# Prompt attention of a one-core hybrid trunk: probabilities scaled before their transposition, values as the stationary operand

## The chip, the cores and the metric

The program runs on one core of a Trainium2 chip. The metric is the time of one execution on the device, in microseconds. The engines of the core are named as the profile names them: PE (TensorE, matrix multiplications and transpositions), DVE (VectorE), ACT (ScalarE), POOL (GpSimd) and SP (the queue that loads the weights). Each runs its own list of instructions in order, and they meet only at semaphores.

## The reference

One layer of a decoder: 512 prompt tokens and 8 sample tokens go through a combined input projection, four mixers (gated linear attention, HGRN2, pooling, sparse attention), gates, an output projection and an MLP. The change lies in the sparse attention of the prompt, and in how its result is handed to the last branch projection:

```
q = rms_norm(heads(nq, H_D), q_ng).reshape(B, L, KVH_D, G_D, HD_D)     # 2 key heads x 4 queries x 64
pc    = masked_softmax(q kc^T, ...);  o_cmp = pc vc                    # 31 compressed blocks
ps    = masked_softmax(q ks^T, ...);  o_slc = ps vs                    # selected blocks
pw    = masked_softmax(q kw^T, ...);  o_win = pw vw                    # window
return gb[..., 0:1] * o_cmp + gb[..., 1:2] * o_slc + gb[..., 2:3] * o_win
...
x = x + einsum(sum_b sigmoid(h W_g + b_g)_b * (o_b W_b), w_out)        # o_nsa is branch b = 3
```

With 512 prompt tokens there are 8 selection blocks, fewer than the 16 to be chosen, and the window is as long as the prompt, so both branches are plain causal attention with their own keys and values.

## The kernel before

All matrices are float32. A projection of the layer is made of three float32r products (high and low parts of weight and input); ACT casts the high part of each 128 x 1024 weight chunk (`upper`, L1151) and POOL subtracts to get the low part (`lower`, L2072). DVE and ACT take the results out of PSUM.

**Compressed branch** (PE L865 to L882). The scores of four query tiles lie in `CM`, 128 x 1024. DVE subtracts the maximum, ACT takes the exponential, DVE sums (L1751), masks with `cmp01` (L1752, which signals `cp`), and afterwards forms 1/sum times the gate in `rsc` (L1754, L1757). PE waits for `cp`, transposes each tile and multiplies it with the block-diagonal compressed values `VBK`: the transposed probabilities are the stationary operand, 256 columns of values move (L878). DVE scales the result with `rsc` on its way from PSUM into `ON`, token-major (L1767).

**The prompt loop.** `PAIRS` (L472) lists 32 pairs: query tile i = 0..3 (the outer loop), branch b (selected, window), and n = 0..3, which stands for two heads, 7-n (key head 1, c = 0) and n (key head 0, c = 1). The loop runs 34 rounds; round p works on three pairs at once:

- PE: a step of the compressed attention of the samples (`compressed_step`); scores of pair p (L972, two heads on two row halves, 128(i+1) columns); then for c = 0, 1: transposition of the probabilities of pair p-1 (`probs_transposed`, L943, i+1 tiles into bank 4), one step of the branch and gate projections (`mix_step`, L809, into the only bank 7), and the product of probabilities and values of pair p-2 (`probs_values`, L956).
- DVE: causal mask (L1888) and maximum (L1890) of pair p; for c = 0, 1 the copy of the transposed probabilities of pair p-1 out of PSUM into `PT` (L1899) and the evacuation of the mix step if it is a branch step (L1676, L1680).
- ACT: the exponentials of pair p with their row sums into `rs` (L1350), then the mix steps of the round: tanh of a gate (L1299) and `upper` of the next chunk (L1151).
- POOL: `lower` after each `upper`, and the gathers of the compressed cache (L2143).

Of every four rounds, the first two hold gate steps (24 matmuls each) and the last two branch steps (12 each). An `upper` falls into three of every four rounds, always beside the round's first mix step: behind its tanh in the second round of the four, right behind the exponentials in the third and fourth. For p below 8 the mix steps also carry the folds of the gathered compressed cache (DVE L1686, L1687, PE L822).

**The product with the values** takes the transposed probabilities (128 keys x 128 tokens) as the stationary operand and 128 columns of values as the moving one, so bank 6 holds eight heads side by side, token-major. The probabilities aren't normalised: after every four pairs (p % 4 == 1, L1906) DVE takes the reciprocal of the row sums, multiplies by the gate (L1909, L1910), scales bank 6 into `TQ` (L1915) and adds it to `ON` (L1916), which signals `on`. The next four pairs may write bank 6 only behind it.

**After the loop** PE waits for the last `on`, transposes `ON` in 16 matmuls (L987), DVE copies them into the feature-major `ONT` (L1919), PE fills a bank with sample values (L994), waits for all four copies, and begins the cache attention of the samples (`keys_transposed`, L1008; `scores`, L1018; `values`, L1039). POOL may gather piece 7 and later of that cache only behind the last `on` (L2168).

## Time and profile before

| | |
|---|---|
| runs | 1409.42, 1410.96, 1417.57 us; median 1410.96 |
| profiled execution | 1409.77 us, of which the span in the profile is 1408.0 us |
| granted PE clock, mean | 0.963 of full speed |
| busy share of the span | PE 91%, DVE 40%, ACT 30%, POOL 36% |
| prompt loop | first scores at 545.78 us, last product with values begins at 817.37 us |
| cache attention of the samples | 825.48 to about 893 us |

The profile is of one execution. Busy time of PE counts overlapping matmuls in a pipeline, so the rate at which matmuls follow each other is read from a run of them: start of the first to end of the last, less the length of one, divided by their number less one. A float32 product is issued as two matmuls.

### The profile page before, as it was taken

To read this page: it belongs to the slowest core of one execution; us is meant where nothing else is said; L and a number is where in the kernel's file an instruction comes from. 1 tells how busy PE (TensorE), PEld (TensorE's weight loads), DVE (VectorE), ACT (ScalarE), POOL (GpSimd) and SP (SyncE) were. 2 spreads that over 40 slices of the span, in tenths; PEclk is the share of its full clock that TensorE was granted. 3 is DMA by queue.
4 is the path that set the end of the run, shared out by engine and by line. 5 is a ranking of instruction groups with operands and counts; after the bars stand their busy time and mean duration, and the time that the engine had idled before them with its cause. 6 is when DMAs were issued, how large, how long until landed. Compare 5 with 4: busy or idle time off the path is not lost.

```text
span 1408.0 us, 24162 instructions
## 1 busy us (share of the span) xinstructions
PE 1279.7 (91%) x10332; PEld 1196.6 (85%) x10332; DVE 568.7 (40%) x853; ACT 416.4 (30%) x647; POOL 502.5 (36%) x262
## 2 busy tenths in 40 slices
PE   4898989998987898888998977889999999999998
PEld 3798888897977887777887855889999999999998
DVE  3544644262425553656667655623122100122002
ACT  3343321013443112223332213333343311234110
POOL 1355533055123334322221235234334444444441
PEclk9899999999998899999999999999999999999999
DMA  4221010632024354431110349232222222222222
GB/s 170 106 91 46 31 60 31 134 96 100 31 92 135 124 177 147 138 105 46 46 61 31 120 160 328 88 130 90 75 89 91 86 94 89 90 90 89 90 90 75
DMA packets 47159, 139.51 MB, mean 99 GB/s; under 512 B 4454, under 2 KB 16074, under 8 KB 46682
## 3 DMA queue, kind: packets, MB, share of 16 engines
q1 hardware_dynamic: 36706, 100.50, 21.5%
q0 software_dynamic: 10368, 37.75, 7.9%
q8 instruction: 68, 1.11, 0.3%
q14 instruction: 17, 0.14, 0.0%
HBM read 129.98 MB, written 8.49 MB: 98 GB/s over the span
## 4 chain that ended last, share of the span: by engine, by line
PE 74%; DVE 12%; DMA 4%; ACT 3%; issue 3%; POOL 2%; DVEq 0%; ACTq 0%
PE PS L598 42%; PE PS L809 10%; PE PS L626 7%; DMA M<-cache_cmp_kv,idx 2%; PE PS L680 2%; PE PS L956 2%; POOL WL L2072 1%; DMA M<-cache_slc_kv,idx 1%; PE PS L943 1%; DVE M L1686 1%; PE PS L1008 1%; PE PS L972 1%; DVE xT L1560 1%; PE PS L584 1%; PE PS L772 1%
## 5 line engine op out<-in xcount | busy, mean ns | idle before, releaser
L2072 POOL TENSOR_TENSOR WL<-M,WH 128x1024 fp32r<-128x1024 f32 x159 | 392.7, 2473 | 759.9 <-ACT WH L1151 759.6
L1151 ACT CAST WH<-M 128x1024 fp32r<-128x1024 f32 x159 | 165.7, 1047 | 280.4 <-DMA M<-weights 280.4
L598 PE MATMUL PS<-hH,WH 128*128 128x260 f32 x1040 | 216.3, 290 | 14.5 <-DVE hL L1448 12.9
L598 PE MATMUL PS<-hL,WH 128*128 128x260 f32 x1040 | 212.6, 287 | 0.0
L598 PE MATMUL PS<-hH,WL 128*128 128x260 f32 x1040 | 212.4, 286 | 0.0
L598 PEld LDWEIGHTS PS<-hH,WH 128*128 128x128 f32 x1040 | 164.1, 193 | 18.8 <-POOL WL L2072 7.6
L598 PEld LDWEIGHTS PS<-hL,WH 128*128 128x128 f32 x1040 | 163.9, 193 | 0.0
L598 PEld LDWEIGHTS PS<-hH,WL 128*128 128x128 f32 x1040 | 163.6, 192 | 0.0
L809 PE MATMUL PS<-hH,WH 128*128 128x260 f32 x384 | 115.6, 301 | 4.4 <-ACT tmp L1299 2.4
L809 PE MATMUL PS<-hL,WH 128*128 128x260 f32 x384 | 111.3, 290 | 0.0
L809 PE MATMUL PS<-hH,WL 128*128 128x260 f32 x384 | 110.9, 289 | 0.0
L598 PE MATMUL PS<-uH,WH 128*128 128x260 f32 x512 | 103.2, 283 | 2.3 <-DVE M L2046 2.3
L598 PE MATMUL PS<-uH,WL 128*128 128x260 f32 x512 | 103.2, 283 | 0.0
L598 PE MATMUL PS<-uL,WH 128*128 128x260 f32 x512 | 103.0, 283 | 0.0
L626 PE MATMUL PS<-WH,hH 128*128 128x256 f32 (+1 forms) x280 | 85.0, 304 | 4.6 <-POOL WL L2072 3.7
L809 PEld LDWEIGHTS PS<-hH,WH 128*128 128x128 f32 x384 | 75.7, 197 | 7.6 <-ACT tmp L1299 4.8
L598 PEld LDWEIGHTS PS<-uH,WH 128*128 128x128 f32 x512 | 78.9, 188 | 2.7 <-issue 2.7
L626 PE MATMUL PS<-WL,hH 128*128 128x256 f32 (+1 forms) x280 | 80.6, 288 | 0.0
L2054 DVE TENSOR_TENSOR M<-M,PS 128x520 f32 x16 | 11.1, 697 | 171.7 <-PE PS L598 171.7
L626 PE MATMUL PS<-WH,hL 128*128 128x256 f32 (+1 forms) x280 | 80.3, 287 | 0.0
L598 PEld LDWEIGHTS PS<-uH,WL 128*128 128x128 f32 x512 | 78.9, 188 | 0.0
L598 PEld LDWEIGHTS PS<-uL,WH 128*128 128x128 f32 x512 | 78.7, 188 | 0.0
(371 smaller groups left out, 2340.8 us busy)
## 6 DMA issues: line engine op xcount, KB each, us to landing
M<-weights SPq DMA_DIRECT2D x159, 512.0 KB, 3.2
M<-cache_win_kv POOLq DMA_DIRECT2D x7, 512.0 KB, 4.3
spill<-xT SPq DMA_DIRECT2D x1, 2080.0 KB, 8.7
M<-spill SPq DMA_DIRECT2D x1, 2080.0 KB, 8.7
M<-x_prompt SPq DMA_DIRECT2D x4, 512.0 KB
y_prompt<-M SPq DMA_DIRECT2D x4, 512.0 KB
con<-tables SPq DMA_DIRECT2D x1, 1437.5 KB, 12.4
M<-state_gla SPq DMA_DIRECT2D x2, 512.0 KB, 6.6
```

Source lines behind the costliest of these rows:

```text
L584: last = mm(PS[:, bank + h, 0:HALF], ones, SQN[k % 2][:, HALF * h:HALF * h + HALF], start=(k == 0), stop=(k == KT - 1))
L598: last = mm(PS[:, bank + h, 0:HALF], w[:, slot_of(n), k, :], x[:, HALF * h:HALF * h + HALF], start=(start and k == k0 and w is WH and x is ...
L626: last = mm(PS[0:m, bank, 0:pieces * cols], x[:, k, t], w[:, n % 4:n % 4 + pieces, k, 0:cols], start=(k == 0 and x is hH and w is WH), sto ...
L680: last = mm(PS[:, bank, 64 * k:64 * k + 64], a, later, start=True, stop=True)
L772: last = mm(PS[:, 2 * (e % 2) + h, 0:HALF], ones if kind == "o" else BO, SQ[e % 2][:, HALF * h:HALF * h + HALF], start=True, stop=True)
L809: last = mm(PS[:, mix_bank(k), 0:HALF], w[:, slot_of(n), at, :], x[:, half], start=(c == 0 and w is WH and x is hi), stop=(c == (KT if gat ...
L943: last = tr(PS[:, 4, 128 * j:128 * j + 128], P[2 * (p % 2) + c][:, 128 * j:128 * j + 128], ident)
L956: last = mm(PS[:, 6, out], PT[2 * (p % 2) + c][:, j], zt[:, j, col:col + out.stop - out.start], start=(j == 0), stop=(j == i))
L972: last = mm(PS[:, 2 * (p % 2) + c, 0:128 * i + 128], QT[r, g, 128 * i:128 * i + 128], (KTS, KTW)[b][r, 0:128 * i + 128], start=True, stop= ...
L1008: last = tr(PS[:, s % 2, 128 * i:128 * i + 128], piece(j, s, i)[0], ident)
L1151: nc.scalar.copy(WH[:, at].rearrange("p k n -> p (k n)"), WR[:, at]).then_inc(sem("w_hi"), 1)
L2072: p.tensor_tensor(WL[:, at].rearrange("p k n -> p (k n)"), WR[:, at], WH[:, at].rearrange("p k n -> p (k n)"), ALU.subtract).then_inc(sem( ...
```

## The change

The row sums of a pair are turned into gate / sum at once, for its two heads, by DVE (`probs_factor`, two small instructions a round). ACT multiplies each head's probabilities by that factor in place (`ACT.Copy` with a per-partition scale, two a round, behind the round's first mix step), and signals `p_norm`, for which the transposition now waits. In the product the values become the stationary operand (128 keys x 64) and the transposed probabilities move; head 7-n writes partitions 64 to 127 of bank 6 and head n partitions 0 to 63, on two column groups of PE, and the matmuls of the two heads alternate. All eight pairs of a query tile, both branches, accumulate in bank 6, feature-major, and DVE adds the bank to `ONT` once per query tile. The compressed branch is treated likewise: `CM` is scaled with `rsc` ahead of `cp`, the product writes feature-major on two column groups in 8 products of 128 columns a tile, and DVE copies it into `ONT`. `ON`, `TQ`, the 16 transpositions and the four copies behind the loop go. The order of the features in `ONT` is another, so the rows of `w_branch[3]` are reordered on the host, and the samples' result goes into `ONT` in two copies, not four.

```diff
@@ PE, compressed branch
-                    for k in range(HKV):
-                        last = mm(PS[:, i - 1, 256 * k:256 * k + 256], PTC[:, i - 1, k], VBK[:, k],
-                                  start=True, stop=True)
+                    for g in range(G):
+                        for k in range(HKV):
+                            last = mm(PS[64 * k:64 * k + 64, i - 1, 128 * g:128 * g + 128], VBK[:, k, 64 * g:64 * g + 64],
+                                      PTC[:, i - 1, k], start=True, stop=True)
@@ PE, prompt loop
             def probs_transposed(p, c):
-                pe.wait_ge(sem("ex"), 2 * p + c + 1)
+                pe.wait_ge(sem("p_norm"), 2 * p + c + 1)
...
-            def probs_values(p, c):
+            def probs_values(p):
                 i, b, heads = PAIRS[p]
-                h = heads[c]
-                pe.wait_ge(sem("pt_ev"), 2 * p + c + 1)
-                if p % 4 == 0 and c == 0 and p:
-                    pe.wait_ge(sem("on"), p // 4)
+                pe.wait_ge(sem("pt_ev"), 2 * p + 2)
+                if p % 8 == 0 and p:
+                    pe.wait_ge(sem("on"), p // 8)
                 col = (CS, CW)[b] + 128
-                out = slice(64 * h - 64 * (h // G), 64 * h - 64 * (h // G) + (64 if h == 3 else 128))
                 for j in range(i + 1):
-                    last = mm(PS[:, 6, out], PT[2 * (p % 2) + c][:, j], zt[:, j, col:col + out.stop - out.start],
-                              start=(j == 0), stop=(j == i))
+                    for c, h in enumerate(heads):
+                        k, g = h // G, h % G
+                        last = mm(PS[64 * k:64 * k + 64, 6, 128 * g:128 * g + 128], zt[:, j, col + 64 * k:col + 64 * k + 64],
+                                  PT[2 * (p % 2) + c][:, j], start=(p % 8 == 0 and j == 0), stop=(p % 8 == 7 and j == i))
                 last.then_inc(sem("pv_mm"), 1)
...
-                    if p >= 2:
-                        probs_values(p - 2, c)
-
-            for i in range(TT):
-                if i == 0:
-                    pe.wait_ge(sem("on"), 2 * TT)
-                for c in range(4):
-                    last = tr(PS[:, i, 128 * c:128 * c + 128], ON[:, i, 128 * c:128 * c + 128], ident)
-                last.then_inc(sem("ont_mm"), 1)
+                    if p >= 2 and c == 0:
+                        probs_values(p - 2)
...
-            pe.wait_ge(sem("ont"), 4)
+            pe.wait_ge(sem("on"), TT)
@@ ACT, prompt loop
                 for k in range(PREP + LOOP * p // 32, PREP + LOOP * (p + 1) // 32):
                     mix_step(k)
+                    if k == PREP + LOOP * p // 32:
+                        act.wait_ge(sem("r_norm"), p + 1)
+                        for c, h in enumerate(heads):
+                            part = P[2 * (p % 2) + c][:, 0:128 * i + 128]
+                            f(part, part, ACT.Copy, scale=rs[:, i, b, h:h + 1]).then_inc(sem("p_norm"), 1)
@@ DVE, compressed branch
-            v.tensor_tensor(CM, CM, C("cmp01")..., ALU.mult).then_inc(once("cp"), 1)
+            step(v.tensor_tensor(CM, CM, C("cmp01")..., ALU.mult))
             step(v.reciprocal(rsc, rsc))
             dve.wait_ge(*done("ng"))
             step(v.tensor_tensor(rsc, rsc, gate[:, 0:4, :, 0], ALU.mult))
+            v.tensor_tensor(cm, cm, bc(rsc.rearrange("p i h -> p (i h)"), 32), ALU.mult).then_inc(once("cp"), 1)
...
-                    v.tensor_tensor(ON[:, i - 1]..., PS[:, i - 1]..., bc(rsc[:, i - 1], HD), ALU.mult)\
+                    v.tensor_copy(ONT[:, :, 128 * i - 128:128 * i], PS[:, i - 1].rearrange("p (g t) -> p g t", g=4))\
                         .then_inc(sem("co_ev"), 1)
@@ DVE, prompt loop
+            def probs_factor(p):
+                i, b, (high, low) = PAIRS[p]
+                both = slice(low, high + 1, high - low)
+                dve.wait_ge(sem("ex"), 2 * p + 2)
+                step(v.reciprocal(rs[:, i, b, both], rs[:, i, b, both]))
+                v.tensor_tensor(rs[:, i, b, both], rs[:, i, b, both], gate[:, i, both, 1 + b], ALU.mult)\
+                    .then_inc(sem("r_norm"), 1)
...
                         if w >= 4:
-                            dve.wait_ge(sem("pv_mm"), w - 3)
+                            dve.wait_ge(sem("pv_mm"), w // 2 - 1)
                         v.tensor_copy(PT[w % 4]..., PS[:, 4, 0:128 * i + 128]).then_inc(sem("pt_ev"), 1)
                         if p < NP and LOOP * p // 32 + c < LOOP * (p + 1) // 32:
                             mix_step(PREP + LOOP * p // 32 + c)
+                        if c == 0 and p < NP:
+                            probs_factor(p)
...
-                if p % 4 == 1 and p > 1:
-                    i, b = PAIRS[p - 2][0:2]
-                    step(v.reciprocal(rs[:, i, b], rs[:, i, b]))
-                    step(v.tensor_tensor(rs[:, i, b], rs[:, i, b], gate[:, i, :, 1 + b], ALU.mult))
-                    dve.wait_ge(sem("pv_mm"), 2 * p - 2)
+                if p % 8 == 1 and p > 1:
+                    i = PAIRS[p - 2][0]
+                    dve.wait_ge(sem("pv_mm"), p - 1)
                     dve.wait_ge(sem("co_ev"), 4)
-                    on = ON[:, i].rearrange("p (h d) -> p h d", d=HD)
-                    t = TQ.rearrange("p (h d) -> p h d", d=HD)
-                    step(v.tensor_tensor(t, PS[:, 6]..., bc(rs[:, i, b], HD), ALU.mult))
-                    v.tensor_tensor(on, on, t, ALU.add).then_inc(sem("on"), 1)
-            for i in range(TT):
-                dve.wait_ge(sem("ont_mm"), TT)
-                v.tensor_copy(ONT[:, :, 128 * i:128 * i + 128], PS[:, i]...).then_inc(sem("ont"), 1)
+                    on = ONT[:, :, 128 * i:128 * i + 128]
+                    v.tensor_tensor(on, on, PS[:, 6].rearrange("p (g t) -> p g t", g=4), ALU.add).then_inc(sem("on"), 1)
@@ POOL, cache of the samples
                 if n == 7:
-                    gp.wait_ge(sem("on"), 2 * TT)
+                    gp.wait_ge(sem("on"), TT)
```

## Rows read from the trace of the kernel before

**Rows 1.** The page's part 4: engines' shares of the chain that ended last.

```profile
PE 74%; DVE 12%; DMA 4%; ACT 3%; issue 3%; POOL 2%; DVEq 0%; ACTq 0%
```

**Rows 2.** Windows of the loop: stretch, length; busy (count) by engine; clock; DMA.

```profile
545.00:611.00 66.00, 55.71 (x383) 47.87 (x382) 41.18 (x77) 17.47 (x47) 25.74 (x16) 0.95 0.43 140
611.00:676.00 65.00, 58.98 (x432) 52.52 (x431) 40.09 (x72) 20.61 (x50) 15.56 (x8) 0.94 0.19 65
676.00:748.00 72.00, 69.29 (x548) 62.59 (x547) 45.60 (x72) 23.59 (x55) 16.09 (x6) 1.00 0.14 45
748.00:821.00 73.00, 65.01 (x492) 56.27 (x492) 50.31 (x71) 18.69 (x41) 16.84 (x11) 1.00 0.23 80
```

**Rows 3.** Waits, 545 to 821 us: who for whom; total us, times, longest.

```profile
ACT M L1350 <- DVE stat L1890: 136.9, 31, 12.8
...
PE PS L943 <- DVE M L1899: 15.2, 13, 4.0
```

**Rows 4.** Timeline, 665 to 671 us, ACT, POOL, DVE: start, length, instruction.

```profile
665.26 0.47 ACT L1350 ACTIVATE M<-PS,stat 128x256 f32<-128x256 f32 x1 [2.49 <-DVE stat L1890]
...
667.30 2.36 POOL L2072 TENSOR_TENSOR WL<-M,WH 128x1024 fp32r<-128x1024 f32 x1 [4.84 <-ACT WH L1151]
...
668.13 1.81 DVE L1680 TENSOR_TENSOR xT<-xT,tmp 128x260 f32<-128x260 f32 x1
...
671.05 0.47 ACT L1350 ACTIVATE M<-PS,stat 128x256 f32<-128x256 f32 x1 [3.83 <-DVE stat L1890]
```

**Rows 5.** Timeline, 817 to 826 us, PE, DVE, POOL: the loop's end.

```profile
817.37 2.00 PE L956 MATMUL PS<-M 128*128 128x128 f32 x16
...
819.46 0.69 DVE L1915 TENSOR_TENSOR M<-PS,stat 128x512 f32<-128x512 f32 x1 [0.77 <-PE PS L956]
820.18 0.69 DVE L1916 TENSOR_TENSOR M<-M 128x512 f32<-128x512 f32 x1
820.93 1.97 PE L987 MATMUL PS<-con,M 128*128 128x128 f32 x16 [1.56 <-DVE M L1916]
821.17 0.56 POOL L2176 DMA_DIRECT2D M<-cache_win_kv  x1 [8.43 <-DVE M L1916]
...
822.83 1.15 PE L994 MATMUL PS<-M 8*128 8x128 f32 x8
...
825.48 0.76 PE L1008 MATMUL PS<-con,M 128*128 128x128 f32 x5 [1.50 <-DVE M L1919]
```

**Rows 6.** Timelines of PE alone, five stretches: runs of matmuls.

```profile
223.92 4.54 PE L701 MATMUL PS<-M,xT 128*64 128x128 f32 x64
...
273.36 3.72 PE L734 MATMUL PS<-M,con 8*64 8x256 f32 x32
...
503.10 1.02 PE L878 MATMUL PS<-M 128*128 128x256 f32 x4
...
792.05 1.05 PE L956 MATMUL PS<-M 128*128 128x128 f32 x8
...
805.02 1.13 PE L972 MATMUL PS<-M 64*128 64x512 f32 x4
806.08 0.65 PE L943 MATMUL PS<-con,M 128*128 128x128 f32 x4
```

**Rows 7.** Timeline, 626 to 634 us, DVE and PE: scaling after four pairs.

```profile
626.49 0.20 DVE L1909 RECIPROCAL stat<-stat 128x8 f32<-128x8 f32 x1
626.73 2.01 DVE L1910 TENSOR_TENSOR stat<-stat,M 128x8 f32<-128x8 f32 x1
...
632.86 0.41 PE L943 MATMUL PS<-con,M 128*128 128x128 f32 x2 [1.35 <-DVE M L1899]
```

**Rows 8.** Line L1910, all of it: count, duration in ns (min/median/max), first and last start.

```profile
L1910 DVE TENSOR_TENSOR stat<-stat,M x8: 170/1556/2207, 595.3 to 818.5; 128x8 f32<-128x8 f32 x8
```

**Rows 9.** Line L1412, all of it: ACT's scaled copy, 520 columns.

```profile
L1412 ACT ACTIVATE hH<-M,small x8: 732/732/733, 977.8 to 1022.5; 128x520 fp32r<-128x520 f32 x8
```

**Rows 10.** Timeline, 469 to 480 us, DVE: masking the compressed probabilities.

```profile
473.05 1.22 DVE L1752 TENSOR_TENSOR M<-M,con 128x1024 f32<-128x1024 f32 x1
```

More of the change, by code:

```diff
@@ L343, in build @@
         zg2 = zf[:, ZG + 4:ZG + 8].rearrange("p a b -> p (a b)")
-        TQ = zk[:, 1100:1612]
         TK = F[:, 0:1280].rearrange("p (i c) -> p i c", i=5)
@@ L353, in build @@
         VBK = zk[:, 0:512].rearrange("p (k c) -> p k c", k=2)
-        ON = zf[:, ZQ:ZQ + 4].rearrange("p a b -> p (a b)")[:, 0:2048].rearrange("p (i c) -> p i c", i=4)
         ONT = zf[:, ZQ:ZQ + 4]
@@ L1751, in _ @@
             step(v.tensor_reduce(rsc.rearrange("p i h -> p (i h)"), cm, AX, ALU.add))
-            v.tensor_tensor(CM, CM, C("cmp01").rearrange("p (i c) -> p i c", i=4).unsqueeze(2)
-                            .to_broadcast([128, 4, 8, 32]), ALU.mult).then_inc(once("cp"), 1)
+            step(v.tensor_tensor(CM, CM, C("cmp01").rearrange("p (i c) -> p i c", i=4).unsqueeze(2)
+                                 .to_broadcast([128, 4, 8, 32]), ALU.mult))
             step(v.reciprocal(rsc, rsc))
@@ L1766, in _ @@
                     dve.wait_ge(sem("co_mm"), i)
-                    v.tensor_tensor(ON[:, i - 1].rearrange("p (h d) -> p h d", d=HD),
-                                    PS[:, i - 1].rearrange("p (h d) -> p h d", d=HD), bc(rsc[:, i - 1], HD), ALU.mult)\
+                    v.tensor_copy(ONT[:, :, 128 * i - 128:128 * i], PS[:, i - 1].rearrange("p (g t) -> p g t", g=4))\
                         .then_inc(sem("co_ev"), 1)
@@ L1902, in _ @@
                             mix_step(PREP + LOOP * p // 32 + c)
+                        if c == 0 and p < NP:
+                            probs_factor(p)
                 elif p == 0:
                     mix_step(PREP)
+                    probs_factor(0)
                 compressed_step(2 * p + 1)
-                if p % 4 == 1 and p > 1:
-                    i, b = PAIRS[p - 2][0:2]
-                    step(v.reciprocal(rs[:, i, b], rs[:, i, b]))
-                    step(v.tensor_tensor(rs[:, i, b], rs[:, i, b], gate[:, i, :, 1 + b], ALU.mult))
-                    dve.wait_ge(sem("pv_mm"), 2 * p - 2)
-                    dve.wait_ge(sem("co_ev"), 4)
-                    on = ON[:, i].rearrange("p (h d) -> p h d", d=HD)
-                    t = TQ.rearrange("p (h d) -> p h d", d=HD)
-                    step(v.tensor_tensor(t, PS[:, 6].rearrange("p (h d) -> p h d", d=HD), bc(rs[:, i, b], HD), ALU.mult))
-                    v.tensor_tensor(on, on, t, ALU.add).then_inc(sem("on"), 1)
-            for i in range(TT):
-                dve.wait_ge(sem("ont_mm"), TT)
-                v.tensor_copy(ONT[:, :, 128 * i:128 * i + 128], PS[:, i].rearrange("p (c t) -> p c t", c=4))\
-                    .then_inc(sem("ont"), 1)
+                if p % 8 == 1 and p > 1:
+                    i = PAIRS[p - 2][0]
+                    dve.wait_ge(sem("pv_mm"), p - 1)
+                    dve.wait_ge(sem("co_ev"), 4)
+                    on = ONT[:, :, 128 * i:128 * i + 128]
+                    v.tensor_tensor(on, on, PS[:, 6].rearrange("p (g t) -> p g t", g=4), ALU.add).then_inc(sem("on"), 1)
             dve.wait_ge(*done("vn_mm"))
@@ L1993, in _ @@
             dve.wait_ge(sem("oacc"), 2)
-            oa = OACC.rearrange("p (s k j q) -> p k q j s", k=2, j=2, q=2)
-            for k in range(2):
-                for q in range(2):
-                    ins = v.tensor_copy(ONT[64 * q:64 * q + 64, 2 * k:2 * k + 2, L:T], oa[64 * k:64 * k + 64, k, q])
-                    if k + q < 2:
-                        step(ins)
-                    else:
-                        ins.then_inc(once("nsa_done"), 1)
+            oa = OACC.rearrange("p (s k g) -> p k g s", k=2, g=G)
+            step(v.tensor_copy(ONT[0:64, :, L:T], oa[0:64, 0]))
+            v.tensor_copy(ONT[64:128, :, L:T], oa[64:128, 1]).then_inc(once("nsa_done"), 1)
             dve.wait_ge(sem("b_hi"), 4)
@@ L2236 @@
     gate = tiles(a["w_gate"][0]).reshape(4, 8, 128, KT, COLS)
-    branch = [a["w_branch"][0, b].reshape(4, 128, 4, 2, COLS).transpose(2, 1, 3, 0, 4).reshape(4, 128, KT, COLS)
+    wb = a["w_branch"][0]
+    wb = np.concatenate([wb[:3], wb[3:].reshape(1, 2, G, HD, D).transpose(0, 2, 1, 3, 4).reshape(1, 512, D)])
+    branch = [wb[b].reshape(4, 128, 4, 2, COLS).transpose(2, 1, 3, 0, 4).reshape(4, 128, KT, COLS)
               for b in range(4)]
```

## Prediction

> **What bounds the kernel now.** I read the chain of waits first: PE holds 74% of it [rows 1], so the question is how much PE time the change removes where PE sets the pace. The windows of the loop come next [rows 2]: PE is busy 55.7 of 66, 59.0 of 65, 69.3 of 72 and 65.0 of 73 us, DVE 41 to 50, ACT 80.4 us of the 276 in all. The clock lies at 0.94 to 1.00 there. No engine but PE is near full, yet PE isn't full either; the waits say why [rows 3]. ACT waits 136.9 us for DVE's maximum, which is slack, but PE waits 15.2 us in 13 stops, at most 4.0, for DVE's copy of the transposed probabilities.
>
> A second pace lies beside PE's. In two branch rounds [rows 4] the exponential starts at 665.26 and the next at 671.05, 5.8 us later: exponentials, ACT's cast, POOL's subtraction (2.36 us from 667.30), and DVE's addition at 668.13, which takes 1.81 us and ends 0.28 after the subtraction; then mask, maximum, exponential. So I treat gate rounds (24 matmuls a step) as bound by PE, branch rounds (12) as bound by that ring, and rounds below 8 by the gathers and folds.
>
> **The end of the loop.** The last product ends at 819.37 and the keys' transposition starts at 825.48, 6.11 us later [rows 5]. In between lie two DVE operations of 0.69, 16 transpositions (1.97) and four copies. After the change there is one DVE addition (about 0.8 with its semaphores) beside the 1.15 us of sample values that PE does anyway. So about 1.2 us are left, a gain of 4.9. POOL's piece 7 starts only 0.7 us sooner relative to the product. So far it is issued 4.3 us ahead of the first keys' transposition, and then 0.4: it is late next. The second job needs it, and the whole first job's transpositions and scores lie in front, so I charge nothing; if that cover fails, at most the 3.9 us come back.
>
> **The products with the values.** 320 matmuls before and after, each with 128 moving columns. Before, eight take 1.05 us, the last 0.27 long: 0.111 us from one to the next [rows 6]. After, 64 columns are stationary and two column groups alternate. The nearest row is L701, same shape: (4.54 - 0.27)/63 = 0.068. The ends: 0.111 if the groups didn't run beside each other, and half of it, 0.0555, by L734, where 256 columns go at (3.72 - 0.37)/31 = 0.108 against 0.214 on the full array (L878). I take 0.068. Against it stands a change of tile shape twice a round: the scores, four matmuls of 512 columns on two row halves, should take 4 x 0.214 = 0.86, and the next transposition starts 1.06 behind them, so 0.2 us for a change in and out. A round with tile i then saves 4(i+1) x 0.043 - 0.2 = -0.03, 0.14, 0.32, 0.49 us. I count the four gate rounds of each i from 1 to 3 (3.8) and the last product (0.5): 4.3. Branch rounds give theirs to the ring. Ends: -2.6 (0.2 lost in 13 rounds), and 6.3 at 0.0555.
>
> "TensorEngine Tiling (Array Packing)", section Theoretical Speedup, of the Trainium skill gives up to 2x for a stationary side of at most 64 columns. By it the term would be the 6.3 of the last end; L701's row gives 1.6x.
>
> **The scaling after four pairs.** Seven of these blocks stand inside the loop. One costs DVE 0.20 for the reciprocal, 2.01 for the product with the gate [rows 7], and 0.69 twice [rows 5]; the product's time is 1.56 in the median of eight and 0.17 at least [rows 8], and behind the block shown PE waits 1.35 [rows 7]. Four blocks go, three shrink to one addition of 0.69. I take 5 us, a third of PE's 15.2 us [rows 3]; ends 0 (the mask was late anyway) and 7 x 1.35 = 9.5.
>
> **The factors.** 32 pairs of small DVE instructions, 0.20 + 0.17 and some 0.08 of semaphores: 0.45 a round, 14 us in all. They wait for both exponentials; behind them on DVE stand the copy of the second head's transposed probabilities, the second mix evacuation and the next mask, and for that copy wait PE's next transposition and product. In gate rounds PE is still at its first mix step then, and that hides them. I charge six rounds where DVE also has folds or sample work: -2.7; ends 0 and -14.
>
> **ACT's scaling.** 64 copies of at most 512 columns, at most 0.73 us each [rows 9], 47 us on top of 80 in 276. It stands behind the first mix step and its cast, in front of the round's second tanh, which waits for a PE step anyway, and `lower` depends on the cast alone. PE needs the result only after its second mix step and the next scores. Nothing; uncovered, one scaling would cost 0.73. The product now waits for both heads' copies, but the next transposition, ahead of it on PE, waits for the same second copy already.
>
> **The compressed branch.** PE: 64 matmuls at 0.068 (4.4 us) for 16 at 0.214 (3.4): -0.9; at 0.0555 it is -0.1. DVE: one more 128 x 1024 product, 1.22 [rows 10], in front of two folds of gathered rows; PE reaches `cp` long after, but the folds feed the gathers. I take -0.8; ends 0 and, if a POOL subtraction holds the second fold, -2.4. Scaling and copy out of PSUM are the same length. The reordered weights are read as before; two sample copies less lie beside PE's projection. The DMA queues issue what they did, in the same order.
>
> **Sum.** 4.9 + 4.3 + 5.0 - 2.7 - 0.9 - 0.8 = 9.8 us less, on the profiled execution's 1409.77 (span 1408.0 and 1.8 around it): 1400.0. The median of the runs is 1.2 us above that execution, so I say **1401 us**, 0.7% less.
>
> **Rivals.**
>
> *All of it arrives.* The groups run fully beside each other and the scaling's whole price goes: 4.9 + 6.3 + 9.5 - 2.7 = 18, less 0.5 for the compressed branch: about 1393. For it: L734's exact half. Against: L701, and PE's waits have other owners too (the casts, the folds).
>
> *The ring takes it.* DVE, ACT and POOL set the pace in most rounds, the products' gain and the scaling's are given back in front of the mask, and only the loop's end stays: 4.9 - 2.7 - 1.7 = 0.5, about 1410. For it: 5.8 us from exponential to exponential [rows 4]. Against: 69.3 of 72 us of PE [rows 2].
>
> *Slower: the factor is held by POOL.* While POOL subtracts, DVE's product with the gate stood for 2.01 us [rows 7], for 1.56 in the median [rows 8]. The new factor is that instruction, 32 times. Three rounds in four have a subtraction, 24 in all; met each time, it costs 1.56 - 0.17 = 1.39 and holds the copy PE waits for: +33 - 9.8, about 1434. It decides where the factor starts after the cast behind the exponentials is done: in a branch round the subtraction begins 2.04 us after the first exponential does [rows 4], and the factor can begin when the second one ends, about a cast earlier. I expect DVE to be there in time in most rounds. Seven collisions on the path cancel the gain, seventeen make 1% slower.
>
> "SBUF — State Buffer", section SBUF: two separate sides, of the Trainium skill describes this as an exclusive lock on a port pair that a DVE operation with two SBUF inputs shares with POOL. The trace agrees: the 2.01 us beside 0.17 undisturbed.
>
> *The groups don't run beside each other.* Then the change doesn't do what it says: -2.6 instead of 4.3, about 1408. L701 and L734 speak against it.
>
> **Chances.** Forecast (1396 to 1407) 0.50, all of it 0.22, the ring 0.17, no overlap 0.05, held factor 0.06. The range 1390 to 1411 takes in the first four but for their edges. A measurement here can't tell less than about 1%, 14 us, from no change: faster (below 1397) is the all-of-it case and an edge of the forecast with better luck in the waits, 0.28; slower (above 1425) the held factor and the unforeseen, 0.07; the same, 0.65.
>
> **What would show it.** The keys' transposition 1.2 us behind the last product; runs of L956's successor at 0.068; PE's waits for the copy below 10 us; factor products at 0.17, not 1.5; no transposition waiting for ACT's scaling. The forecast is wrong if branch rounds don't get shorter where a scaling block went, or if the cache attention of the samples, once begun sooner, waits longer for piece 7.

## The result, and the profile after

| | before | after | after, a second measurement |
|---|---|---|---|
| median | 1411.64 us (4 runs) | 1397.47 us (4 runs) | 1400.98 us (6 runs; 1412.53 before) |
| ratio to before, 95% interval | | 0.9895 [0.9861, 0.9928] | 0.9928 [0.9901, 0.9955] |
| profiled execution / its span | 1409.77 / 1408.0 | 1399.79 / 1397.8 | 1394.77 / 1392.8 |

The change makes the kernel faster by 14.8 and 10.2 us by the two ratios, 14.2 and 11.6 by the medians, about 0.9%. 1401 had been predicted, and 1396 to 1407 as the range of the forecast's own case. The sum holds; what follows is mostly about its terms, which don't hold as well.

The page of the changed kernel, part 4. The chain is still PE's, with the same 74% [rows 1]:

```profile
PE 74%; DVE 11%; DMA 5%; ACT 3%; issue 3%; POOL 3%; DVEq 0%; ACTq 0%
```

Windows of its loop, from just before its first scores to the keys' transposition. The inner cuts stand at the times of [rows 2], and the first two lie 5 and 2 us of work earlier than there; the last window of [rows 2] ends 4.5 us ahead of the keys' transposition. Stretch, length; busy (count) of PE, PE's weight loads, DVE, ACT, POOL; clock; DMA share; GB/s.

```profile
553.00:611.00 58.00, 52.89 (x378) 45.07 (x377) 37.79 (x80) 21.69 (x61) 23.55 (x16) 0.97 0.41 134
611.00:676.00 65.00, 55.86 (x421) 47.31 (x420) 39.90 (x87) 27.22 (x67) 15.73 (x9) 0.95 0.22 78
676.00:748.00 72.00, 68.86 (x555) 58.06 (x554) 45.13 (x85) 33.48 (x74) 16.52 (x7) 0.98 0.15 52
748.00:818.00 70.00, 63.95 (x509) 52.11 (x507) 47.02 (x76) 27.72 (x55) 17.54 (x13) 0.95 0.24 84
```

ACT has 110 us of work in place of 80, DVE 170 in place of 177, and yet the loop, from its first scores to the keys' transposition, takes 264.2 us in place of 279.7. The clock is lower than before in the last two windows; that comes back below.

Waits from 553.5 to 816.5 us (who for whom; total us, times, longest), beside [rows 3]:

```profile
ACT M L1342 <- DVE stat L1896: 102.9, 31, 13.2
PE PS L942 <- DVE M L1905: 9.9, 8, 3.2
PE PS L942 <- ACT M L1351: 2.6, 1, 2.6
```

PE's wait for the copy of the transposed probabilities went from 15.2 to 9.9 us. ACT's scaling (L1351) is waited for once, in round 11, where other work of ACT (two table loads of 1.28 us for the samples) stands ahead of it; in the kernel before, PE waited 4.0 us for the copy in that round.

To say where the time went, I cut each profile at five starts that all kernels have: the scores of the compressed branch, the first scores of the loop, the scores of round 9, those of round 31, the keys' transposition, and at the projection behind the cache attention. Lengths in us; A to E name the stretches from here on:

| kernel | A compressed | B rounds 0 to 8 | C rounds 9 to 30 | D round 31 to the keys | E cache attention |
|---|---|---|---|---|---|
| before | 85.4 | 75.0 | 184.2 | 20.5 | 67.6 |
| after | 88.9 | 71.8 | 177.3 | 15.2 | 64.6 |
| after, second | 86.0 | 71.3 | 177.3 | 15.4 | 66.6 |
| heads in turn | 88.3 | 75.0 | 179.0 | 14.1 | 65.6 |
| one group | 89.7 | 72.7 | 183.1 | 14.5 | 64.8 |
| scaling back | 87.8 | 75.5 | 181.8 | 15.6 | 65.7 |
| end back | 87.7 | 72.9 | 177.4 | 21.1 | 66.2 |
| no factors | 87.7 | 71.0 | 177.3 | 15.3 | 66.6 |
| ACT twice | 89.6 | 72.8 | 177.3 | 15.5 | 66.5 |
| mask first | 88.2 | 73.0 | 175.8 | 15.0 | 67.4 |
| compressed back | 85.2 | 75.1 | 177.4 | 15.4 | 67.7 |
| compressed wide | 87.4 | 71.5 | 177.3 | 15.4 | 67.4 |
| before, no scaling | 85.2 | 71.9 | 179.9 | 19.7 | 66.3 |
| before, no end | 85.5 | 74.7 | 184.3 | 15.9 | 68.6 |

C is read from starts like these, of the scores of round 9 before and after, and of round 31 after (805.02 before, [rows 6]):

```profile
620.80 0.70 PE L972 MATMUL PS<-M 64*128 64x256 f32 x4
```

```profile
625.54 0.70 PE L971 MATMUL PS<-M 64*128 64x256 f32 x4
802.81 1.13 PE L971 MATMUL PS<-M 64*128 64x512 f32 x4
```

A profile is one execution, so the first thing to read is how far a stretch moves where nothing in it was changed. C is the same within 0.2 in seven of the eight profiles whose loop differs by nothing or by the factors or ACT alone (175.8 in the eighth, mask first, of which more at the end), D within 0.3 where the end is the same. B is not: 71.0 to 75.1 in the same eight profiles. E goes mostly with the clock: 64.6 and 64.8 us at a mean of 0.97 and 0.98, 66.2 to 66.6 at 0.92 to 0.94, 67.6 and 68.6 at 0.91 and 0.92; but 66.2 and 68.6 stand at the same 0.92, so the clock isn't all of it. So C and D carry the argument, A and B only in the mean, and the 3 us that E is shorter after the change are put down to the execution.

Inside C most rounds of these eight profiles agree within 0.1 us, each from its scores to the next. Three places don't: rounds 11 and 12 trade up to 1.2 us with each other and rounds 27 and 28 up to 1.3 (each pair's sum is the same within 0.1), and round 24 is 8.6 us in mask first and 10.0 to 10.2 in the other seven. Where differences by single rounds are given below, the two pairs that trade are left out. In B, round 6 agrees as well (5.25 to 5.28).

The span went from 1408.0 to 1397.8: 4.6 us were lost ahead of A, in unchanged work (the clock was 0.74 in the first 60 us, 0.86 in the profile before), A +3.4, B to D -15.5, E -3.0, the rest +0.4.

### The profile page after: what moved, and what is told of

Its sections match the earlier page's. It is cut to its first block, busy times and chain, and to the rows that moved or that the text cites. A ratio compares the mean times of both kernels' runs of the same rounds, so it can differ in the third digit from the quotient of the medians.

```text
span 1397.8 us, 24312 instructions
## 1 busy us (share of the span) xinstructions
PE 1275.1 (91%) x10364; PEld 1182.8 (85%) x10364; DVE 559.7 (40%) x884; ACT 446.0 (32%) x711; POOL 501.7 (36%) x262
## 4 chain that ended last, share of the span: by engine, by line
PE 74%; DVE 11%; DMA 5%; ACT 3%; issue 3%; POOL 3%; DVEq 0%; ACTq 0%
PE PS L596 43%; PE PS L807 10%; PE PS L624 7%; DMA M<-cache_cmp_kv,idx 3%; DMA M<-cache_slc_kv,idx 2%; PE PS L678 2%; PE PS L942 1%; POOL WL L2067 1%; PE PS L582 1%; PE PS L971 1%; PE PS L955 1%; DVE xT L1557 1%; PE PS L1000 1%; PE PS L770 1%; PE PS L714 1%
```

## Experiments

Every kernel's ratio is to the kernel before, measured beside it on the same chip.

**The changed kernel again**, for the noise.

> The changed kernel once more, unaltered, on the chip of the runs beside it. It tells which differences between the two profiles belong to the change and which to the execution. If the account by stages holds: first 60 us and everything up to the compressed scores within 5 us either way with the granted clock, loop (first scores to the keys' transposition) 264 us +-2, cache attention of the samples (keys' transposition to the first product of the projection behind it) 64.5 us. Rival: the 3.0 us less in the cache attention (67.5 to 64.5) were luck of the clock; then this run has 66 to 68 there.

1400.98 us, 0.9928. The loop takes 263.9 us, as expected (264.2 in the first profile); A is 86.0 and not 88.9, E 66.6 and not 64.6. The rival was right on E.

**The alternation of the heads.**

```diff
                 for j in range(i + 1):
                     for c, h in enumerate(heads):     # changed kernel
---
                 for c, h in enumerate(heads):         # heads in turn
                     for j in range(i + 1):
---
-                        last = mm(PS[64 * k:64 * k + 64, 6, ...   # one group
+                        last = mm(PS[0:64, 6, ...
```

> The changed kernel, but in the product with the values all tiles of one head come first and then those of the other, so neighbouring matmuls use the same column group. If the alternation is what brings the rate: 0.107 to 0.111 us from one matmul to the next instead of 0.055. Theory of the forecast (only gate rounds of query tiles 1 to 3 are bound by PE): 4 rounds x (8 + 12 + 16) matmuls x 0.055 = 7.9 and 0.9 for the last product, so the loop takes 8 to 9 us more. Rival, PE is the bound in all rounds: 320 x 0.055 = 17.6 more. Rival, the ring of mask and exponential sets the pace everywhere: 0 to 2 more. Rival, the order does not matter for the rate: 0.

> The changed kernel with both heads of a pair on the same column group (and on the same half of bank 6, so their sums are mixed): the products have no neighbour to run beside. A block of 16 should then take 15 x 0.107 + 0.27 = 1.87 us and not 1.09, one of 12, 8 and 4 take 0.57, 0.36 and 0.16 more: 15 us of PE in 32 blocks. If only the gate rounds of tiles 1 to 3 count, as forecast, 4 x 1.71 + 0.8 = +7.6 in the loop; if PE is the bound in all rounds, +15; if the ring sets the pace, 0 to +2. The heads in turn had 0.49 and 0.26 more a block of 16 and 12, 6.0 in all, and a loop 4.1 longer, two thirds: by that +10.

0.9914 [0.9881, 0.9947] and 0.994 [0.9919, 0.9961]. Blocks of 16 products and the transposition behind them, as PE's timeline has them (start, length, instruction), in the changed kernel:

```profile
791.16 1.09 PE L955 MATMUL PS<-M 128*64 128x128 f32 x16
792.19 0.66 PE L942 MATMUL PS<-con,M 128*128 128x128 f32 x4
```

with the heads in turn:

```profile
792.94 1.58 PE L955 MATMUL PS<-M 128*64 128x128 f32 x16
```

and on one group:

```profile
803.34 0.28 PE L807 MATMUL PS<-bX,WL 128*128 128x260 f32 x1
803.55 1.96 PE L955 MATMUL PS<-M 128*64 128x128 f32 x16
805.44 0.66 PE L942 MATMUL PS<-con,M 128*128 128x128 f32 x4
```

The rates are (1.09 - 0.27)/15 = 0.055, 0.087 and 0.113 us. On one group C takes 5.9 us more, 4.7 of them in its gate rounds and 1.2 in its branch rounds. The blocks in C grew by 0.2, 8 x 0.43, 8 x 0.64 and 5 x 0.87 = 13.1, so 45% counted. Without the rounds that trade, gate rounds took on 3.6 of 4.9 and branch rounds 2.2 of 5.6, so the forecast's rule that gate rounds count and branch rounds don't holds only by half. With the heads in turn C takes 1.8 more. The rest of its loop's 4 us lies in B (+3.4, with D -1.2), and B moves that far by itself, so the two thirds that I had worked out of its loop for the next expectation were chance.

**The scaling blocks.** Put back into the changed kernel, and taken out of the kernel before:

```diff
+                if p % 4 == 1 and p > 1:                        # scaling back
+                    ...
+                    step(v.reciprocal(t[:, 0:8], rs[:, i, b]))
+                    step(v.tensor_tensor(t[:, 0:8], t[:, 0:8], gate[:, i, :, 1 + b], ALU.mult))
+                    dve.wait_ge(sem("pv_mm"), p - 1)
+                    step(v.tensor_tensor(t..., PS[:, 6]..., bc(rs[:, i, b], HD), ALU.mult))
+                    if p % 8 == 5:
+                        v.tensor_tensor(t, t, t, ALU.add).then_inc(sem("four"), 1)
---
-                if p % 4 == 1 and p > 1:                        # before, no scaling
-                    step(v.reciprocal(...)); step(v.tensor_tensor(rs..., gate..., ALU.mult))
+                if p % 8 == 1 and p > 1:
-                    step(v.tensor_tensor(t, PS[:, 6]..., bc(rs[:, i, b], HD), ALU.mult))
-                    v.tensor_tensor(on, on, t, ALU.add).then_inc(sem("on"), 1)
+                    v.tensor_tensor(on, on, PS[:, 6]..., ALU.add).then_inc(sem("on"), 1)
```

> The changed kernel with the work of the scaling blocks put back every four pairs: reciprocal of 8, product of 8 with the gate, product of bank 6 with a broadcast factor into scratch, and in the middle of a query tile an addition in scratch for which the next product waits. Bank 6 is restarted there, so the first branch is left out of the result. Forecast: +5.0 in the loop (a third of PE's waits for the copy), ends 0 and +9.5. Rival: the blocks were covered by the late mask: 0 to +1. Rival: they cost what they last and what POOL holds of them, 7 x about 3.4 = 24, less what PE has in stock: +10 or more.

> The kernel before without the scaling blocks: no reciprocal, no product with the gate, no scaling of bank 6, and only one addition of bank 6 to ON per query tile (normalisation, gate and the first branch are left out of the result). Forecast: -5.0 in the loop, ends 0 and -9.5. Putting the blocks back into the changed kernel cost 8.8; if the price is the same on both sides, -8.8. Rival: in the kernel before, the mask was late anyway and the loop's pace is the ring's: 0 to -2.

0.9979 [0.9959, 0.9999] and 0.9947 [0.9925, 0.9969]. Both ways agree in C, +4.5 and -4.3. B has +3.9 against the two profiles of the changed kernel and -3.1, but only one of the seven blocks, that of round 5, lies in it; round 6, behind that block, gives +1.1 and -1.2, and the rest is what B moves by itself. That is 5.5 to 5.7 us in the rounds that repeat. By the medians of the kernels measured together it is 7.8 and 8.4; the second ratio leaves 4.4 to 10.6. (D's -0.8 is the one DVE operation less at the loop's end, 6.11 to 5.33, and counts there.) Of C's 4.3, 3.5 are in branch rounds, and all but 0.1 without the rounds that trade: the block ends a gate round and stands in front of the mask of the next, a branch round.

Rounds 6, 10, 18 and 26 have most of it: 1.2, 0.8, 1.2 and 1.2 us shorter without the blocks, and 1.1 to 1.2 each longer with them put back. Behind the blocks of rounds 13, 21 and 29 the next two rounds change by 0.8 at most. The length of the block doesn't decide it: in the first kernel the product with the gate takes 0.17 us in rounds 5, 9, 17 and 25 and 1.81, 1.93 and 0.88 in 13, 21 and 29. What differs is DVE's other work around the block: in the kernel before 2.1 to 4.6 us (folds, work for the samples, the low part of a projection's input) in rounds 5, 9, 17 and 25, and at most 0.7 in the other three, where in rounds 13 and 21 the block itself waits for PE's product. PE's wait for the copy in round 26 of the kernel before, with the blocks and without:

```profile
763.49 0.63 PE L943 MATMUL PS<-con,M 128*128 128x128 f32 x4 [2.04 <-DVE M L1899]
```

```profile
758.44 0.63 PE L943 MATMUL PS<-con,M 128*128 128x128 f32 x4 [0.88 <-DVE M L1899]
```

PE's waits for the copy in the loop of the changed kernel with the blocks, and in the kernel before without them:

```profile
PE PS L942 <- DVE M L1907: 13.8, 11, 3.2
```

```profile
PE PS L943 <- DVE M L1899: 9.7, 8, 4.0
```

9.9 without the blocks and 13.8 with them, 15.2 with and 9.7 without: 3.9 to 5.5 of these waits were the blocks', about a third, as the forecast had it, and near the 5.5 to 5.7 that the rounds show. DVE's groups in the first of the two kernels (shape, count | busy, mean ns of one); the product with the gate takes 0.68 in the mean there and 1.24 in the kernel before, at the same price:

```profile
L1923 DVE TENSOR_TENSOR M<-PS,stat 128x512 f32<-128x512 f32 x8 | 5.5, 692 | 1.0 <-PE PS L957 0.8
L1921 DVE TENSOR_TENSOR M<-M 128x8 f32<-128x8 f32 x8 | 5.5, 683 | 0.3
```

**The loop's end**, put back into the changed kernel (transpositions of ONT, copies into scratch), and left out of the kernel before:

```diff
+            for i in range(TT):                                  # end back
+                if i == 0:
+                    pe.wait_ge(sem("on"), TT)
+                for c in range(4):
+                    last = tr(PS[:, i, 128 * c:128 * c + 128], ONT[:, c, 128 * i:128 * i + 128], ident)
+                last.then_inc(sem("ont_mm"), 1)
---
-            pe.wait_ge(sem("ont"), 4)                            # before, no end
+            pe.wait_ge(sem("on"), 2 * TT)
```

> The changed kernel with 16 transpositions of ONT, four copies of 128x512 out of PSUM (into scratch, each behind the one before) and the wait for them put back behind the loop. Forecast of the loop's end: the keys' transposition begins 6.1 us behind the last product and not 2.0, so +4.1 to +4.9 and nothing more. Rival: the idle time of PE there also lowers the granted clock in the cache attention, as in the kernel before (0.56 to 0.58 for 8 us): then 3 more behind it, +7 in all. Rival: the later piece 7 of the cache was hiding a part: +2.

> The kernel before without the 16 transpositions and four copies behind the loop (so the projection reads values that were not transposed). Forecast: the keys' transposition begins 1.2 us behind the last product instead of 6.1, -4.9. By the changed kernel's trace it is 1.9 (the sample values take their time there), so -4.2. Putting them back into the changed kernel cost 5.7 (its copies were chained one behind the other) and nothing in the cache attention. Rival: the idle time also lowered the clock in the cache attention: then 1 to 3 less there too (67.5 to 65).

0.9949 [0.9929, 0.997] and 0.9982 [0.9966, 0.9998]. From the last product's end to the keys: 1.93 to 7.64 (D +5.7), and 6.11 to 1.56 (D -4.6). The end put back costs more than it did before, since its transpositions take 3.68 us at the lower clock, for 1.97, and its copies, chained, 3.08, for 2.49. With the end put back, and in the kernel before without it:

```profile
812.10 1.97 PE L955 MATMUL PS<-M 128*64 128x128 f32 x16
814.87 3.68 PE L986 MATMUL PS<-con,M 128*128 128x128 f32 x16 [0.79 <-DVE M L1927]
818.58 3.08 DVE L1933 COPY M<-PS 128x512 f32<-128x512 f32 x4 [3.77 <-PE PS L986]
821.71 1.46 PE L1007 MATMUL PS<-con,M 128*128 128x128 f32 x8 [1.90 <-DVE M L1933]
```

```profile
821.09 2.00 PE L956 MATMUL PS<-M 128*128 128x128 f32 x16
824.65 1.09 PE L1001 MATMUL PS<-con,M 128*128 128x128 f32 x8 [0.48 <-DVE M L1909]
```

E stays where the changed kernel's other profiles have it, and in the kernel before it did not get shorter (68.6): no price of the end beyond itself shows.

**The factors and ACT's scaling.**

```diff
-                dve.wait_ge(sem("ex"), 2 * p + 2)                # no factors
-                step(v.reciprocal(rs[:, i, b, both], rs[:, i, b, both]))
-                v.tensor_tensor(rs[:, i, b, both], ..., gate[:, i, both, 1 + b], ALU.mult)...
---
-                            f(part, part, ACT.Copy, scale=rs[:, i, b, h:h + 1]).then_inc(sem("p_norm"), 1)
+                            step(f(part, part, ACT.Copy, scale=rs[:, i, b, h:h + 1]))   # ACT twice
+                            f(part, part, ACT.Copy, scale=1.0).then_inc(sem("p_norm"), 1)
```

> The changed kernel without the two small DVE instructions a round that form gate / sum; ACT scales by the raw row sums instead, so the gate and the normalisation are left out of the result. Forecast: the factors cost 2.7, so the loop (264 us) gets 2.7 shorter; ends 0 (gate rounds hide them all) and -14 (they lie on the path in each round). In the trace of the changed kernel DVE waits 12.0 us in 14 stops for the exponentials ahead of the reciprocal, and the copy of the second head's probabilities stands behind it: if that wait is on the path, -6 or more. Rival: the price of the factor is what POOL holds, one 2.3 us in one of two profiles, so -1 or less.

> The changed kernel with each of ACT's 64 scalings done twice (the second by 1.0), and the second signals the transposition. Forecast: ACT's scaling is hidden, so doubling it costs nothing in the loop (264 us), 0 to +1. Rival: the transposition already waits for it (2.6 us in one stop in the changed kernel's trace), and each more microsecond of ACT in front of it is paid in the rounds that are short: 64 x 0.2 to 0.7 us, about 30 us of ACT, of which a third on the path, +10. Rival, partly covered: the exponentials of the next pair stand behind it, +2 to +4.

0.9895 [0.9867, 0.9924] and 0.9906 [0.9885, 0.9926]. Without the factors C is 0.1 longer and the loop 0.3 to 0.6 shorter: they cost nothing in C. In B, where the rounds with folds lie that the forecast charged, 71.0 stands beside 71.3 and 71.8, less than B moves by itself. The 12 us in which DVE waits ahead of the reciprocal are slack. The line of the factor's product in the first profile of the changed kernel, and in the second (count: min/median/max in ns, first and last start):

```profile
L1882 DVE TENSOR_TENSOR stat<-stat,M x32: 162/165/2316, 557.6 to 807.4; 128x2 f32<-128x2 f32 x32
```

```profile
L1882 DVE TENSOR_TENSOR stat<-stat,M x32: 162/164/165, 552.7 to 801.3; 128x2 f32<-128x2 f32 x32
```

One collision with POOL's subtraction in 64. In the ten profiles of kernels with the factors it is five in 320, all five in the loop's second round. Doubling ACT's part adds some 30 us to ACT and 0.1 to C; the 1.7 by which the loop is longer lie in B. It is hidden.

**The compressed branch.** Its products as before (wide), and those and the scaling as before (back):

```diff
-                    for g in range(G):                           # wide, back
-                        for k in range(HKV):
-                            last = mm(PS[64 * k:64 * k + 64, i - 1, 128 * g:128 * g + 128], VBK[:, k, 64 * g:64 * g + 64],
-                                      PTC[:, i - 1, k], start=True, stop=True)
+                    for k in range(HKV):
+                        last = mm(PS[:, i - 1, 256 * k:256 * k + 256], PTC[:, i - 1, k], VBK[:, k], start=True, stop=True)
-            v.tensor_tensor(cm, cm, bc(rsc..., 32), ALU.mult).then_inc(once("cp"), 1)           # back
```

> The changed kernel with its compressed branch computed as in the kernel before: 16 products of 256 columns on the full array, no scaling of CM ahead of them (the result of this branch is not scaled and lies in the wrong order, so it is not the reference's). The stage from the compressed scores to the first scores of the loop took 85.3 to 85.5 in three profiles of kernels with the old branch and 86.0 to 89.7 in nine with the new one. If the new branch costs it: 85.3 to 85.6 here. If the length is chance of the granted clock: 86 to 89 here too. The loop stays at 264 +-1 in both.

> The changed kernel with only the products of the compressed branch as before (16 of 256 columns on the full array, so the layout of this branch's result is not the reference's), while DVE still scales CM ahead of them. If DVE's additional product (1.23 us ahead of the folds) is what lengthens the stage: 86 to 89. If the 64 narrow products are (1.09 a tile for 1.02, and what they do to the clock): 85.3 to 85.6.

0.9911 [0.9892, 0.993] and 0.9915 [0.9887, 0.9944]. Windows of stretch A, in the kernel before, the first and second profile of the changed one, compressed back, compressed wide:

```profile
460.34:545.78 85.44, 74.01 (x526) 69.68 (x525) 41.21 (x71) 15.07 (x21) 36.52 (x25) 0.92 0.45 148
```

```profile
464.94:553.79 88.85, 77.29 (x574) 71.86 (x573) 41.99 (x72) 15.06 (x21) 37.02 (x25) 0.88 0.44 143
```

```profile
462.18:548.17 85.99, 74.74 (x574) 69.50 (x573) 41.55 (x72) 15.06 (x21) 36.95 (x25) 0.92 0.45 146
```

```profile
465.20:550.43 85.23, 74.01 (x526) 69.68 (x525) 40.64 (x71) 15.07 (x21) 36.55 (x25) 0.92 0.44 148
```

```profile
465.91:553.34 87.43, 75.45 (x525) 71.12 (x525) 43.92 (x72) 15.08 (x21) 37.13 (x25) 0.90 0.44 145
```

A is 85.2 to 85.5 in four profiles with the old branch and 86.0 to 89.7 (mean 88.2) in the eight of kernels with the new one unaltered. With the scaling alone it is 87.4, inside that range, so the narrow products aren't needed for most of it, and the scaling ahead of the folds is. The clock of the stretch is 0.88 to 0.92, mostly lower where A is longer, but A is 88.3 at 0.92 with the heads in turn. Whether the 2.9 reach the end is open: the changed kernel with the old branch put back gave them back in B (75.1; A and B together 160.3, against 157.3 to 162.5 with the new branch and the same loop), where the folds wait for the same gathers, and its time is that of the changed kernel.

**A version with both ends mended.**

```diff
-            step(v.tensor_tensor(CM, CM, C("cmp01")..., ALU.mult))
+            step(v.tensor_tensor(rsc, rsc, C("cmp01")...[:, :, 0:1].to_broadcast([128, 4, 8]), ALU.mult))
...
+                    if p == NP + 1 and c == 0:      # sample values, into bank 3, ahead of the last product
```

> The changed kernel with two small edits. The mask of the compressed probabilities goes into the 128x32 factor (a token that sees any block sees block 0), so one 128x1024 product of DVE (1.23 us) goes from in front of the folds. The sample values are multiplied into bank 3 ahead of the last product instead of behind it. Expected if the compressed part is paid by the folds it delays: that stage like the kernel before, 85.3 to 85.6, against 86.0 to 89.7 in the changed kernel and its variants; and the keys' transposition 1.0 us behind the last product instead of 1.9 (the addition alone is in between). Together 1.5 to 4 us less than the changed kernel. Rival: the stage's length goes by the granted clock in its waits for gathered rows, not by DVE: 86 to 89 as before; then 1 us less in all.

0.9919 [0.9899, 0.9939], no faster than the changed kernel. The keys start 0.8 behind the last product, where 1.0 was expected, but the product itself starts that much later, D is 15.0. A is 88.2: one 1.2 us product less on DVE ahead of the folds didn't bring the stretch back, so the rival is right here, and what in the scaling lengthens A isn't settled.

## Why the prediction was right

| step | forecast, us | measured, us | from |
|---|---|---|---|
| loop's end | 4.9 | 4.2 (4.6 and 5.7 by undoing) | last product to keys, D |
| scaling after four pairs | 5.0 (0 to 9.5) | 5.5 to 5.7; 7.8 and 8.4 by medians | C 4.3 and 4.5, round 6 1.2 and 1.1 |
| products with the values | 4.3 (-2.6 to 6.3) | about 3.6 | C 7.0 less the scaling's 4.3, and 0.9 in D |
| factors | -2.7 (0 to -14) | 0, in B within its scatter | C, no factors |
| ACT's scaling | 0 | 0 | C, ACT twice |
| compressed branch | -1.7 | -2.9, perhaps given back | A |
| sum | 9.8 | 11.6 and 14.2 | medians |

**The end** came as forecast but for 0.7. In the changed kernel's timeline (start, length, instruction), beside [rows 5]:

```profile
814.28 1.77 PE L955 MATMUL PS<-M 128*64 128x128 f32 x16
815.98 2.07 PE L986 MATMUL PS<-M 8*128 8x128 f32 x8
816.09 0.69 DVE L1920 TENSOR_TENSOR M<-M,PS 128x512 f32<-128x512 f32 x1 [0.79 <-PE PS L955]
817.08 0.56 POOL L2171 DMA_DIRECT2D M<-cache_win_kv  x1 [6.52 <-DVE M L1920]
817.98 1.97 PE L1000 MATMUL PS<-con,M 128*128 128x128 f32 x8
```

The sample values take 2.07 in place of 1.15 and the last product 1.77 in place of 1.09: the granted clock is at the lower level (0.50) from 815 on. That is where the 0.7 went: with the heads in turn and on one group the clock is 1.00 in D, and the keys start 1.01 behind the last product. Piece 7 is issued 0.9 ahead of the keys' transposition (4.3 before; the forecast's 0.4 should have been 0.1 by its own terms, 4.3 + 0.7 - 4.9), and PE's waits for pieces of the cache in E are 8.2 us in place of 7.9: nothing to charge, as forecast.

**The scaling** came near its 5.0, and by the mechanism that it was priced by: 3.9 to 5.5 us of PE's named waits for the copy went, and the rounds that repeat show 5.5 to 5.7. Branch rounds did get shorter where a block went, the sign that the forecast had asked for. The end of 9.5 took each block for the 1.35 us of [rows 7]; of that wait 0.57 stays in round 10 without any block, and three of the seven blocks cost little, those that have little other work of DVE around them. That this work makes the difference is read from the timelines; no run moves it. The medians, at 7.8 and 8.4, leave room for more, but no stretch that repeats shows it, so this part of *All of it arrives* is neither shown nor excluded. POOL's hold, the 2.01 us of [rows 7], is no part of the price that shows: the blocks of rounds 9 and 17 cost no less with a product of 0.17 than with one of 2.0.

**The products** ran at 0.055, the end of the range and not the 0.068 that I took. *TensorEngine Tiling (Array Packing)*, section Theoretical Speedup, of the Trainium skill gives up to 2x; 0.113 on one group against 0.055 agrees. My row, L701, was the wrong one: it does eight products on one group and then eight on the other, as the heads in turn do (0.087 there). But the time gained was no larger for it. The change of shape is paid in each round, as the forecast had it, about 0.24 us: a block begins 0.21 behind the last projection matmul, where those follow each other at 0.12, and the transposition 1.03 behind the start of the block, not 16 x 0.055 = 0.88. So PE's time on the blocks fell by 4(i+1) x 0.056 - 0.24 a round, 8.4 us in C. Of these 2.7 arrived (7.0 - 4.3), and 4.2 in mask first (179.9 - 175.8), where round 24 has the full clock: about half, near the 45% of one group. The half isn't where my rule put it: against the kernel before without scaling, mask first is 2.2 us shorter in gate rounds and 1.8 in branch rounds, and I had counted gate rounds in full and branch rounds not at all. The product of the second head also no longer stands between two branch steps; on one group, with that order and no faster product, the branch rounds read in the same way are 0.4 longer, so nothing shows a gain by that order, but no run separates it.

**The factors.** *Held by POOL* needed seven collisions to cancel the gain and seventeen to make the kernel 1% slower, and had one in 64. When POOL holds one, it takes 2.1 to 2.3 us in place of 0.16. *SBUF — State Buffer*, section SBUF: two separate sides, of the Trainium skill describes the lock; the trace agrees. The charge of 2.7 for rounds with folds was a cost without a place: taking the factors out gave back at most 0.6 of the loop.

**The ring takes it** is refuted by C: 7 us went, in rounds 9 to 30 alone. **The groups don't run beside each other**: the one-group kernel is that case, and its 1403.7 us, 0.994, shows that it would still have been faster, by the scaling and the end.

So the mechanism of the three gains holds, and the sum is right partly by luck, because errors offset: 0.5 too little for the scaling and 2.7 too much for the factors on one side, 1.2 for the compressed branch, 0.7 for the products and 0.7 for the end on the other. 9.8 + 3.2 - 2.6 = 10.4, or 13.3 if the 2.9 of the compressed branch come back in B. The clock's 1.5 us in round 24 was in no term of the forecast; it lies in the products' 3.6.

## What to carry to other kernels

Price a block on an engine that sits off the chain by the waits that name it, place by place, and not by one wait times the number of blocks: here 3.9 to 5.5 us of named waits stood for 5.5 to 5.7, and seven times the wait shown would have been 9.5. Look at what else the engine has to do around each block. When two heads share PE by column groups, alternate them matmul by matmul; the order alone is worth a factor of 1.6 in the rate of a block of 16 (1.8 us of C here, too little for the medians). And before a difference between two profiles is explained, measure how far each stretch moves with the same code: here one moved by 0.2 us in seven profiles of eight, and its neighbour by 4. Where the rounds of a loop repeat, compare round by round.

## What the hardware showed that I had not expected

The overlap of two column groups reaches only a little ahead in the order of the instructions. With four products of one head and then four of the other a block of 8 still takes 0.66 to 0.67 us, as alternated; with six and six, 1.14 against 0.88; with eight and eight, 1.58 against 1.09.

Some clock was lost in the loop. From 676 us to the end of the loop of the kernel before, PE had the full level throughout [rows 2]; in the changed one the same windows stand at 0.98 and 0.95. There are two stretches of 3 to 4 us at the lower level, from 739 at the start of round 24 and from 773 ahead of round 28, and a third at the loop's end. The first, in windows of 4 us (columns as above), stands behind small matmuls of the sample work:

```profile
735.00:739.00 4.00, 4.00 (x33) 3.77 (x33) 3.39 (x7) 2.54 (x6) 2.35 (x1) 1.00 0.26 85
739.00:743.00 4.00, 4.00 (x17) 2.44 (x17) 2.12 (x4) 0.19 (x1) 0.00 (x0) 0.57 0.11 46
743.00:747.00 4.00, 4.00 (x40) 3.69 (x40) 1.00 (x4) 2.96 (x7) 0.00 (x0) 1.00 0.02 4
```

The four scores of 512 columns there take 1.86 us in place of the 1.13 of [rows 6]. What the two stretches cost can be read from the one kernel with the same loop that has neither, mask first. Its window of the same scores, and the scores in PE's timeline:

```profile
738.50:742.50 4.00, 4.00 (x30) 3.19 (x30) 2.33 (x4) 0.94 (x3) 0.00 (x0) 1.00 0.15 60
```

```profile
738.65 1.13 PE L971 MATMUL PS<-M 64*128 64x512 f32 x4
```

There the clock is 1.00 from 650 to 810 us, and C is 175.8 and not 177.3. Round 24 has all of it: 8.6 us, against 10.0 to 10.2. The second stretch makes round 27 longer and round 28 shorter by as much (10.3 and 11.0 us, against 9.4 and 11.9), and costs nothing. So 1.5 us of the gain went back to the clock in C, in the profiles that have the first stretch.

What brings the stretches on isn't shown. It isn't simply that PE has less to do: mask first has the same loop and neither stretch, and on one group, where the products take as long as before, both are there. The first of them on one group:

```profile
742.00:746.00 4.00, 4.00 (x16) 2.73 (x17) 2.12 (x3) 0.67 (x2) 0.00 (x0) 0.57 0.07 25
```
